# Expert retrieval of 64 of 256 tokens moved from the dense product to indirect row fetches; the first dense table in unsplit fp32

## The chip, the cores and the metric

One NeuronCore of a Trainium2 chip runs the whole layer. The metric is the device time of one execution in microseconds; of several runs the median is taken. The engines are PE (TensorE, matrix products), DVE (VectorE), ACT (ScalarE), POOL (GpSimd) and SP (SyncE, which here only issues DMAs). They run side by side and meet in semaphores.

## What is computed

The reference is one transformer layer over 256 latent tokens of width 1024 with 256 context tokens beside them. After the mixers and the output projection comes the part that the change is about, an expert layer (PEER): each token picks, for each of 8 heads, 16 of 16384 experts, each of which is one row of a table `peer_u` and one row of a table `peer_v`.

```
s = einsum('thpd,hpkd->thpk', h2 @ w_q, sub_keys)      # 2 lists of 128 scores for each head
top 16 of each list, their 256 sums, top 16 of these   -> expert (t, 8, 16), best_s
g   = softmax(best_s)
act = gelu(einsum('thkd,td->thk', u_tab[expert], h2))
out = einsum('thk,thkd->td', g * act, v_tab[expert])
x   = rmsnorm(x + g2 * out)
```

All of it is in fp32, and both tables are 16384 x 1024, 64 MB each.

## The kernel before, in words

The kernel doesn't fetch rows. It streams both tables whole and multiplies them by all 256 tokens, and a matrix of gates, zero nearly everywhere, picks out the experts that a token chose. A table is cut into 128 chunks of 128 rows (512 KB each), and SP brings each chunk into one of the four slots of `stage`.

The order of the work on each engine is written out by hand, in the order of the program text, and every engine runs its list strictly in that order:

- **Prologue** (to about 319 us). Modulation, input projection, attention, output projection, then `w_q` blocks 0 to 7, whose products become queries, and `keys(h)`, which scores the keys of head h. `schedule()` lists these steps for PE, ACT and DVE. POOL computes the low halves of the last five `w_q` blocks. DVE starts on the choice of experts while PE is still at the later `w_q` blocks: `choose(h, ...)` finds the best 16 of two lists of 128 and then the best 16 of 256 sums, for head h and both halves (128 tokens each) of the tokens.
- **u stage** (chunks 0 to 63 of `peer_u`). A product in full fp32 takes two passes on PE at half speed. So each operand is split in a high and a low half of type fp32r, which PE takes in one pass: ACT writes `hi` from `stage` (`round_chunk`), DVE writes `lo = stage - hi` (`rest`), and PE makes three products, hi x hi, hi x lo and lo x hi, for each of the eight blocks of 128 of the contraction (`u_chunk`: 24 matmuls with 256 columns). ACT turns the result into gelu and puts it in `A3[:, c, :]`. DVE goes on with the choice for heads 4 to 7, with one `rest` between any two of its steps, then finds the chosen indices (`BIG`, "decode"), and with ACT the softmax. At chunk `TURN_AT` (60) PE transposes the indices and gates.
- **Merge stage** (chunks 64 to 127 of `peer_u`). For each group of `GT` = 4 tokens ACT and DVE build two one-hot matrices for each token (`one1_...`, `one2`), PE multiplies them (`gates`, four fp32 products of 128x128x128), and DVE multiplies the 4x128 gates into `A3` (`gate`). There are 64 groups for the 64 chunks left, one beside each chunk. DVE also multiplies each late chunk into its place (`multiply`).
- **v stage** (128 chunks of `peer_v`). Again in split form: ACT writes `w_hi` from `A3` (`w_round`), DVE `w_lo` (`w_rest`), and for each half of the tokens and each half of the 1024 columns PE makes three products of 512 columns (`v_chunk`: 12 matmuls), summed over all chunks in banks 4 to 7.
- **Tail.** DVE adds `g2` times the sum to x (`residual`), ACT and DVE make the last norm, and SP stores.

The lines that the text below speaks of: `u_chunk` matmuls are L788 to L790, `gates` L798, `v_chunk` L851 to L853; ACT's rounding of stage L939 and of A3 L1117; DVE's `rest` L1306, `one2` L1495, `gate` L1503, `w_rest` L1535, `residual` L1561; the first step of `choose` L1261, its sums L1277; the decode L1454 to L1463; POOL's subtraction L1594 and its memsets L1598 and L1600.

Of the kernel before, what the change touches and what calls it, by code (L numbers as in the profile page):

```python
# [12 lines left out]
P = 128  # L33
D = 1024
# [19 lines left out]
PIECE = D // 2  # L54
PIECES = 4
GT = 4
GROUPS = T // GT


EARLY = 4  # L60
BESIDE = 8
TOPK_UNTIL = BESIDE * (PH - EARLY)
DECODE_UNTIL = TOPK_UNTIL + 24
SOFTMAX_UNTIL = DECODE_UNTIL + 4
TURN_AT = SOFTMAX_UNTIL
# [17 lines left out]
def schedule():  # L83
# [81 lines left out]
    for b in range(PH):  # L165
        steps.append(("w_q", b))
        turn()
        if b == 6:
            steps.append(("first_chunks", 0))
# [34 lines left out]
def bank_uses(steps):  # L204
# [12 lines left out]
    for kind, n in steps:  # L217
# [27 lines left out]
        elif kind in ("squares", "split", "context", "ctx_squares", "yn", "quarter", "first_chunks"):  # L245
# [10 lines left out]
def build(nc, x_t, ctx_t, cols, rows, sgu_gain, final_gain, constants, sgu_wt, bias_mask, ada_w, w_in,  # L256
          w_out, w_q, subkeys_t, peer_u_t, peer_v, out):
# [20 lines left out]
    with ExitStack() as stack:  # L278
# [10 lines left out]
        with ExitStack() as views:  # L289
            def view(name, size):  # L290
                return views.enter_context(nc.sbuf_tensor(name, [P, size], F32R))
# [12 lines left out]
        A = sbuf("A", [P, CHUNKS * T])  # L304
        A3 = A[:, :].rearrange("p (c t) -> p c t", t=T)

# [49 lines left out]
        assert 24576 == SCRATCH * T  # L356
# [7 lines left out]
        hi = sbuf("hi", [P, PIECES, PIECE], F32R)  # L364
        lo = sbuf("lo", [P, PIECES, PIECE], F32R)
# [4 lines left out]
        x1n = sbuf("x1n", [P, TB, D])  # L370
        YN_lo = yn_low[:, :].rearrange("p (k t) -> p k t", k=KD)
# [13 lines left out]
        w_hi = h2_hi[:, 0:2, :]  # L385
        w_lo = h2_lo[:, 0:2, :]
# [10 lines left out]
        choice_t = sbuf("choice_t", [P, 3, T])  # L397
        gelu_buf = choice[:, 0:2, :, :].rearrange("p n b t -> p n (b t)")
        con = sbuf("con", [P, 5 * P + 2])
        ident, ones, group_ones, iota, row_ones = (con[:, n * P:(n + 1) * P] for n in range(5))  # L400
        row_pick = con[:, 5 * P:5 * P + 2]
        colv = sbuf("colv", [P, COLS])
# [37 lines left out]
        hi_made, lo_made, piece_done, a_made = map(sem, ("hi_made", "lo_made", "piece_done", "a_made"))  # L440
# [32 lines left out]
        def _(sp):  # L473
# [33 lines left out]
            with sp.Fori(1, CHUNKS // SLOTS) as i:  # L507
                for j in range(SLOTS):
                    sp.wait_ge(lo_made, i * (2 * SLOTS) + (2 * (j + 1 - SLOTS)))
                    sp.dma_start(stage[:, j, :], peer_u_t[i * SLOTS + j]).then_inc(stage_full[j], 16)  # L510
            with sp.Fori(0, CHUNKS // SLOTS) as i:
                for j in range(SLOTS):
                    sp.wait_ge(lo_made, i * (2 * SLOTS) + (2 * (CHUNKS + j + 1 - SLOTS)))
# [11 lines left out]
        def _(pe):  # L525
# [192 lines left out]

            def queries(b):
# [21 lines left out]
            for kind, n in steps:  # L741
# [24 lines left out]
                elif kind in ("squares", "split", "context", "ctx_squares", "yn", "quarter", "first_chunks"):  # L766
# [907 lines left out]
```

## Time and profile before

| | |
|---|---|
| three runs | 1107.93 us median (1102.68 to 1108.59) |
| profiled execution, first to last instruction | 1106.2 us |
| PE busy | 1072.4 us, 97% |
| DVE, ACT, POOL busy | 760.1, 628.5 and 37.1 us |
| HBM read | 190 MB, 173 GB/s over the span |
| chunks 0 to 63 of peer_u | 319.4 to 505.7 us |
| chunks 64 to 127 with the gates | 505.7 to 746.9 us |
| peer_v | 748.0 to 1096.5 us |

The profile was taken of an execution of its own, and what is known of its time is its span; it lies within the three runs, 1.7 us under their median. Matmuls are pipelined: a matmul's own duration in the profile (283 ns for one of 256 columns) is longer than the distance from its start to the start of the next one, and it is the distance that adds up.

### The profile page before, as it was taken

The page shows a single profiled execution, that of the slowest core. Times are in us where ns is not written, and L with a number is a line of the kernel's source. Part 1 is how long each engine was busy: PE and PEld are TensorE (multiplying, and loading weights), DVE is VectorE, ACT ScalarE, POOL GpSimd, SP SyncE. Part 2 cuts the span into 40 slices and gives each one's busy share as a digit, 9 for nine tenths or more (in the row PEclk, how much of TensorE's full clock was granted, in tenths as well). Part 3 has the DMA queues.
Part 4 walks back from the last instruction along what each step waited for, and adds up shares of the span by engine and source line. Part 5 has one row for each costly group of instructions (what it writes and reads, how often), then busy time and mean ns, then how long its engine had stood idle before and what let it go on. Part 6 is the DMA issues. An engine that isn't in the chain of part 4 may idle for free.

```text
span 1106.2 us, 22735 instructions
## 1 busy us (share of the span) xinstructions
PE 1072.4 (97%) x7358; PEld 962.5 (87%) x7358; DVE 760.1 (69%) x1660; ACT 628.5 (57%) x1319; POOL 37.1 (3%) x11
## 2 busy tenths in 40 slices
PE   5899999999999999999999999999999999999996
PEld 3687986797999999999999999997888888888885
DVE  1373145576988878868888888886666666666666
ACT  2452235545345555578888888875555555555554
POOL 0000000003340000020000000000000000000000
PEclk9698998999999999999999999999999999999998
DMA  9665741044525555555344344445555666666653
GB/s 362 274 234 197 268 159 57 1 154 152 228 78 190 175 188 173 187 183 161 133 140 144 133 140 144 133 133 174 196 197 192 190 191 192 194 197 192 190 191 113
DMA packets 45547, 191.65 MB, mean 173 GB/s; under 512 B 5186, under 2 KB 5314, under 8 KB 38980
## 3 DMA queue, kind: packets, MB, share of 16 engines
q1 hardware_dynamic: 45508, 191.11, 50.9%
q8 instruction: 26, 0.43, 0.2%
q14 instruction: 13, 0.11, 0.0%
HBM read 190.04 MB, written 1.05 MB: 173 GB/s over the span
## 4 chain that ended last, share of the span: by engine, by line
PE 92%; ACT 3%; DMA 2%; DVE 2%; POOL 0%; issue 0%; DVEq 0%; SPq 0%; ACTq 0%
PE bank L788 11%; PE bank L789 11%; PE bank L790 11%; PE bank L851 10%; PE bank L853 10%; PE bank L852 10%; PE bank L798 5%; PE bank L546 3%; PE bank L547 3%; PE bank L548 3%; PE bank L669 2%; PE bank L566 1%; PE bank L652 1%; PE bank L651 1%; PE bank L660 1%; PE bank L556 1%
## 5 line engine op out<-in xcount | busy, mean ns | idle before, releaser
L939 ACT ACTIVATE hi<-stage 128x512 fp32r<-128x512 f32 x512 | 305.7, 622 | 119.6 <-PE bank L790 119.5
L1306 DVE TENSOR_TENSOR lo<-stage,hi 128x512 fp32r<-128x512 f32 x512 | 336.2, 695 | 33.9 <-ACT hi L939 31.4
L788 PE MATMUL bank<-h_hi,hi 128*128 128x256 f32 x1024 | 295.1, 288 | 1.0 <-ACT A L1062 1.0
L790 PE MATMUL bank<-h_hi,lo 128*128 128x256 f32 x1024 | 289.6, 283 | 0.0
L789 PE MATMUL bank<-h_lo,hi 128*128 128x256 f32 x1024 | 289.5, 283 | 0.0
L851 PE MATMUL bank<-hi,h_hi 128*128 128x512 f32 x512 | 199.3, 389 | 1.2 <-DVE h_lo L1535 1.2
L853 PE MATMUL bank<-hi,h_lo 128*128 128x512 f32 x512 | 199.2, 389 | 0.0
L852 PE MATMUL bank<-lo,h_hi 128*128 128x512 f32 x512 | 199.2, 389 | 0.0
L788 PEld LDWEIGHTS bank<-h_hi,hi 128*128 128x128 f32 x1024 | 196.1, 192 | 1.1 <-ACT A L1062 1.1
L789 PEld LDWEIGHTS bank<-h_lo,hi 128*128 128x128 f32 x1024 | 196.3, 192 | 0.0
L790 PEld LDWEIGHTS bank<-h_hi,lo 128*128 128x128 f32 x1024 | 196.0, 191 | 0.0
L1117 ACT ACTIVATE h_hi<-A 128x256 fp32r (+1 forms) x128 | 53.5, 418 | 162.4 <-PE bank L853 159.5
L1535 DVE TENSOR_TENSOR h_lo<-A,h_hi 128x256 fp32r<-128x256 f32 x128 | 54.5, 426 | 129.4 <-ACT h_hi L1117 129.4
L851 PEld LDWEIGHTS bank<-hi,h_hi 128*128 128x128 f32 x512 | 96.1, 188 | 21.2 <-issue 1.4
L852 PEld LDWEIGHTS bank<-lo,h_hi 128*128 128x128 f32 x512 | 96.1, 188 | 20.1
L853 PEld LDWEIGHTS bank<-hi,h_lo 128*128 128x128 f32 x512 | 96.1, 188 | 19.9
L1081 ACT ACTIVATE gate_buf<-con,choice_t 128x128 f32<-128x128 f32 x256 | 81.2, 390 | 0.0
L548 PE MATMUL bank<-h_hi,ring_low 128*128 128x256 f32 x256 | 72.6, 284 | 0.0
L1495 DVE TENSOR_SCALAR gate_buf<-con,choice_t 128x128 f32<-128x128 f32 x256 | 71.0, 340 | 0.0
L798 PE MATMUL bank<-gate_buf 128*128 128x128 f32 x512 | 67.6, 275 | 0.0
L798 PEld LDWEIGHTS bank<-gate_buf 128*128 128x128 f32 x512 | 62.8, 192 | 0.0
L1503 DVE TENSOR_TENSOR A<-A,bank 128x512 f32 (+1 forms) x64 | 43.9, 687 | 10.4 <-PE bank L798 1.8
(222 smaller groups left out, 1365.8 us busy)
## 6 DMA issues: line engine op xcount, KB each, us to landing
stage<-in_peer_u_t SPq DMA_DIRECT2D x128, 512.0 KB, 3.3
stage<-in_peer_v SPq DMA_DIRECT2D x128, 512.0 KB, 3.6
A<-in_ada_w SPq DMA_DIRECT2D x24, 1024.0 KB, 7.5
A<-in_w_in SPq DMA_DIRECT2D x11, 1024.0 KB, 4.8
A<-in_w_q SPq DMA_DIRECT2D x8, 1024.0 KB, 5.2
A<-in_w_out SPq DMA_DIRECT2D x4, 1024.0 KB, 7.3
stage<-in_bias_mask SPq DMA_DIRECT2D x1, 2048.0 KB, 12.9
A<-in_x_t SPq DMA_DIRECT2D x1, 1024.0 KB, 5.3
```

What stands on the lines that cost most here:

```text
L548: mm = pe.matmul(o, a_lo, b_hi, start=False, stop=(k == KD - 1))
L788: pe.matmul(o, hi[:, p, kk], h2_hi[:, k, :], start=(k == 0), stop=False)
L789: pe.matmul(o, hi[:, p, kk], h2_lo[:, k, :], start=False, stop=False)
L790: mm = pe.matmul(o, lo[:, p, kk], h2_hi[:, k, :], start=False, stop=(k == KD - 1))
L798: mm = pe.matmul(bank[4 + j][:, t * NK:(t + 1) * NK], ONE1[:, j, t, :], ONE2[:, j, t, :], start=True, stop=True)
L851: pe.matmul(o, w_hi[:, j % 2, tt], hi[:, p, :], start=first, stop=False)
L852: pe.matmul(o, w_hi[:, j % 2, tt], lo[:, p, :], start=False, stop=False)
L853: mm = pe.matmul(o, w_lo[:, j % 2, tt], hi[:, p, :], start=False, stop=last)
L939: act.activation(hi[:, (2 * j + h) % PIECES, :], stage[:, j, h * PIECE:(h + 1) * PIECE], ACT.Copy)\
L1081: last = act.activation(ONE1[:, j % 2, t, :], iota, ACT.Square, bias=choice_t[:, 0, bass.ds(g * GT + t, 1)])
L1306: dve.tensor_tensor(lo[:, p, :], stage[:, j, h * PIECE:(h + 1) * PIECE], hi[:, p, :].bitcast(F32), ALU.subtract).then_inc(lo_made, 1)
L1495: last = dve.tensor_scalar(ONE2[:, j % 2, t, :], iota, choice_t[:, 1, bass.ds(tt, 1)], choice_t[:, 2, bass.ds(tt, 1)], ALU.is_equal, ALU.mult)
```

## The change

192 tokens (`ND`) stay in the dense product, and the last 64 take another way. These 64 are two sets (`SUBS`) of 32 (`SUB`).

- **Rows.** 32 tokens with 128 experts each are laid out as 128 partitions with 32 columns: partition q*32+t holds experts of token t. Once the second half of the tokens has its experts (`expert`), POOL copies the indices into that layout (eight small DMAs) and issues an indirect DMA for each column: 128 rows of 4 KB, one for each partition, 512 KB in all. There are 64 such gathers of `peer_u` and 64 of `peer_v`, in a ring of four buffers. DVE multiplies and sums a gathered row of `peer_u` with the token's row of h2 (`row_dots`, one instruction with 1024 elements), and adds a weighted row of `peer_v` to a running sum (`row_sums`, one instruction too). h2 in row form comes from PE (`rows_turned`, four steps between `w_q` 3 and 4).
- **Order on DVE.** `choose` now takes two heads of one half of the tokens, so that the second half can be finished first. 64 `row_dots` stand between the steps of the choice for the first half, and all of them ahead of the first `one2`. The 64 `row_sums` stand in the merge stage (three of four groups, from group 14) and in the v stage (every third chunk).
- **u.** PE multiplies `stage` itself by `H2` in unsplit fp32, 192 columns. `round_chunk` and `rest` of `peer_u` fall away, and with them `first_chunks`; SP's slot comes free when PE has read it.
- **Gates.** 48 groups; merging starts at chunk 80 (`MERGE` = 128 - 48).
- **v.** The first 128 tokens as before with three products. The other 64 share a matmul: the high and the low half of their weights stand side by side as 128 stationary columns, so two products do. That makes 10 matmuls in place of 12. In the end the two halves and the row sums are folded by fp32 products.
- **Memory.** A moves by 8192 elements. `v_hi` and `v_lo` have four buffers of a whole row.

```diff
-EARLY = 4
-BESIDE = 8
-MERGE = 64
-SCRATCH = 96
+SUB = 32
+SUBS = 2
+ND = T - SUB * SUBS
+ND1 = ND - P
+ROWS = PH // 4 * TOPK
+DOTS = SUBS * ROWS
+GROUPS = ND // GT
+MERGE = CHUNKS - GROUPS
+SCRATCH = (24576 - A_AT) // ND
+EXP_AT = 44
+TURN_AT = 60
+GELU_AT = 12
+WEIGH_AT = 14
...
+        if b == 3:
+            steps += [("rows_turned", n) for n in range(2 * SUBS)]
...
+        gathered = [A[:, a:a + D] for a in (2048, 3072, 6144, 7168)]
...
+            def turned_rows(n):
+                o = opened(pe, ("rows_turned", n))
...
+                    for q in range(4):
+                        mm = pe.matmul(o[q * SUB:(q + 1) * SUB, m * P:(m + 1) * P], H2[:, k, tokens], ident,
+                                       start=True, stop=True, tile_position=(0, q * SUB))
...
-            def u_chunk(j, c):
-                o = bank[j % SLOTS][:, 0:T]
-                for h in range(2):
-                    pe.wait_ge(lo_made, c * 2 + (h + 1))
-                    for n in range(KD // 2):
-                        k, p, kk = KD // 2 * h + n, (2 * j + h) % PIECES, slice(n * P, (n + 1) * P)
-                        pe.matmul(o, hi[:, p, kk], h2_hi[:, k, :], start=(k == 0), stop=False)
-                        pe.matmul(o, hi[:, p, kk], h2_lo[:, k, :], start=False, stop=False)
-                        mm = pe.matmul(o, lo[:, p, kk], h2_hi[:, k, :], start=False, stop=(k == KD - 1))
-                    mm.then_inc(piece_done, 1)
+            def u_chunk(j, fill):
+                o = bank[j % SLOTS][:, 0:ND]
+                pe.wait_ge(stage_full[j % SLOTS], fill)
+                for k in range(KD):
+                    mm = pe.matmul(o, stage[:, j % SLOTS, k * P:(k + 1) * P], H2[:, k, 0:ND],
+                                   start=(k == 0), stop=(k == KD - 1))
+                mm.then_inc(u_read, 1)
...
+                        if tb == 0:
+                            pe.matmul(o, w1[:, 0:P], v_hi[j][:, hh], start=first, stop=False)
+                            pe.matmul(o, w1[:, 0:P], v_lo[j][:, hh], start=False, stop=False)
+                            mm = pe.matmul(o, w2[:, 0:P], v_hi[j][:, hh], start=False, stop=last)
+                        else:
+                            pe.matmul(o, w12, v_hi[j][:, hh], start=first, stop=False)
+                            mm = pe.matmul(o, w12, v_lo[j][:, hh], start=False, stop=last)
...
+            for half in range(2):
+                hh = slice(half * 512, half * 512 + 512)
+                for s in range(SUBS):
+                    rows = slice(ND1 + s * SUB, ND1 + (s + 1) * SUB)
+                    pe.matmul(bank[half][rows, :], fold4, sums[s][:, hh], start=True, stop=True,
+                              tile_position=(0, ND1 + s * SUB))
+            for half in range(2):
+                hh = slice(half * 512, half * 512 + 512)
+                pe.wait_ge(rest_out, half + 1)
+                pe.matmul(bank[half][0:ND1, :], fold2, rest[:, hh], start=True, stop=True,
+                          tile_position=(0, 0)).then_inc(folded, 1)
...
+            def row_dots(n):
+                s, c = n // ROWS, n % ROWS
+                g = gathered[n % GATHER]
+                dve.wait_ge(row_full[n % GATHER], 16 * (n // GATHER + 1))
+                dve.tensor_tensor_reduce(g, g, h2_rows[:, s, :], 1.0, 0.0, ALU.mult, ALU.add, row_dot[:, s, c:c + 1])\
+                   .then_inc(row_used, 1)
...
+                    dve.scalar_tensor_tensor(sums[s][:, :], g, w, sums[s][:, :], ALU.mult, ALU.add)\
+                       .then_inc(row_used, 1)
...
+            choose(TB - 1, PH - 2, lambda at: None)
+            decode(TB - 1, lambda: None)
+            dve.scalar_tensor_tensor(expert, choice[:, 0, TB - 1, :], float(NK), choice[:, 1, TB - 1, :],
+                                     ALU.mult, ALU.add).then_inc(expert_ready, 1)
+            for h in range(2, PH, 2):
+                choose(0, h, lambda at: row() if h > 2 or at > 3 else None)
+            decode(0, row)
             dve.sem_inc(scratch_free, 1)
+            row()
             dve.wait_ge(exped, 1)
...
+            row(12)
...
+            row(DOTS - rows_done[0])
...
+                if g == WEIGH_AT:
+                    weigh_rows()
+                if g >= WEIGH_AT and g % 4 < 3:
+                    row()
...
+            for v in range(2, CHUNKS):
+                w_rest(v)
+                if v + 2 < CHUNKS:
+                    rest_of_v(v + 2)
+                if v % 3 == 2:
+                    row()
...
+            def gather(n):
+                s, c, slot = n % DOTS // ROWS, n % ROWS, n % GATHER
+                if n >= GATHER:
+                    pool.wait_ge(row_used, n + 1 - GATHER)
+                pool.indirect_dma_start(gathered[slot], None, peer_u if n < DOTS else peer_v,
+                                        bass.IndirectOffsetOnAxis(ap=row_expert[:, s, c:c + 1], axis=0))\
+                    .then_inc(row_full[slot], 16)
...
+            pool.wait_ge(expert_in, 16 * 4 * SUBS)
+            for n in range(32):
+                gather(n)
             pool.wait_ge(scratch_free, 1)
             pool.memset(A3[:, SCRATCH:CHUNKS, :], 1.0).then_inc(ones_made, 1)
+            for n in range(32, DOTS):
+                gather(n)
```

## Rows read from the trace of the kernel before

**Rows 1.** Page, part 1: busy time, share of the span, instructions.

```profile
PE 1072.4 (97%) x7358; PEld 962.5 (87%) x7358; DVE 760.1 (69%) x1660; ACT 628.5 (57%) x1319; POOL 37.1 (3%) x11
```

**Rows 2.** Busy time by stretch; behind POOL: granted clock, DMA share, GB/s.

```profile
300.00:304.00 4.00, 3.77 (x31) 2.19 (x31) 3.90 (x25) 3.17 (x5) 3.97 (x2) 1.00 1.03 421
319.40:505.70 186.30, 185.33 (x1546) 185.16 (x1545) 152.75 (x363) 107.86 (x207) 13.90 (x2) 1.00 0.54 176
505.70:746.90 241.20, 241.14 (x2049) 240.94 (x2047) 212.48 (x503) 196.18 (x503) 0.00 (x0) 1.00 0.43 139
748.00:1096.50 348.50, 348.43 (x1536) 288.31 (x1536) 218.98 (x385) 187.20 (x385) 0.00 (x0) 1.00 0.58 188
```

**Rows 3.** Waits of PE from 319 to 1097 us: total, times, longest.

```profile
PE bank L851 <- DVE h_lo L1535: 1.2, 1, 1.2
PE bank L788 <- ACT A L1062: 1.0, 1, 1.0
```

**Rows 4.** Timeline of PE: start, duration, line, count.

```profile
247.24 3.85 PE L708 MATMUL bank<-A,con 128*128 128x256 f32 x16
252.76 1.07 PE L566 MATMUL bank<-A,csil 128*32 128x256 f32 x16
...
641.22 1.05 PE L798 MATMUL bank<-gate_buf 128*128 128x128 f32 x8
...
644.98 1.06 PE L798 MATMUL bank<-gate_buf 128*128 128x128 f32 x8
```

**Rows 5.** Timeline of PE's weight loads for unsplit fp32 products.

```profile
247.12 1.61 PEld L708 LDWEIGHTS bank<-A,con 128*128 128x128 f32 x8
...
701.36 0.98 PEld L798 LDWEIGHTS bank<-gate_buf 128*128 128x128 f32 x8
```

**Rows 6.** DVE by line and shape: busy us, mean ns, idle before.

```profile
L1306 DVE TENSOR_TENSOR lo<-stage,hi 128x512 fp32r<-128x512 f32 x512 | 336.2, 695 | 33.9 <-ACT hi L939 31.4
L1495 DVE TENSOR_SCALAR gate_buf<-con,choice_t 128x128 f32<-128x128 f32 x256 | 71.0, 340 | 0.0
L1535 DVE TENSOR_TENSOR h_lo<-A,h_hi 128x256 fp32r<-128x256 f32 x128 | 54.5, 426 | 129.4 <-ACT h_hi L1117 129.4
L1503 DVE TENSOR_TENSOR A<-A,bank 128x512 f32 x60 | 41.2, 687 | 8.5
...
L1454 DVE TENSOR_TENSOR A<-A,con 128x2048 f32<-128x2048 uint32 x4 | 9.1, 2285 | 0.0
...
L1573 DVE SCALAR_TENSOR_TENSOR x1n<-x1n,fsum,gate_buf 128x512 f32<-128x512 f32 x4 | 2.8, 746 | 0.1
```

**Rows 7.** ACT by line and shape, same columns.

```profile
L939 ACT ACTIVATE hi<-stage 128x512 fp32r<-128x512 f32 x512 | 305.7, 622 | 119.6 <-PE bank L790 119.5
...
L1117 ACT ACTIVATE h_hi<-A 128x256 fp32r x124 | 51.8, 418 | 156.1 <-PE bank L853 156.1
```

**Rows 8.** Timeline of DVE: two first steps of `choose`, its sums once, `residual`.

```profile
272.11 3.90 DVE L1277 TENSOR_TENSOR A<-top_v 128x256 f32<-128x256 f32 x2
...
290.90 0.87 DVE L1261 MAX8 top_v<-A 128x8 f32<-128x128 f32 x4
...
301.08 0.87 DVE L1261 MAX8 top_v<-A 128x8 f32<-128x128 f32 x4
...
1097.15 0.68 DVE L1561 TENSOR_TENSOR A<-bank,g2b 128x512 f32<-128x512 f32 x1
```

**Rows 9.** Timeline of POOL; its second subtraction.

```profile
270.79 4.59 POOL L1594 TENSOR_TENSOR ring_low<-A,query_hi 128x2048 fp32r<-128x2048 f32 x1 [1.54 <-ACT query_hi L956]
```

**Rows 10.** POOL by line and shape: the second memset.

```profile
L1600 POOL MEMSET A<- 128x8192 f32 x1 | 7.0, 6954 | 148.2 <-DVEq L1465 148.2
```

**Rows 11.** Page, part 6: DMA issues, count, KB each, us to landing.

```profile
stage<-in_peer_u_t SPq DMA_DIRECT2D x128, 512.0 KB, 3.3
stage<-in_peer_v SPq DMA_DIRECT2D x128, 512.0 KB, 3.6
```

More of the change, by code:

```diff
@@ L256, in build @@
 def build(nc, x_t, ctx_t, cols, rows, sgu_gain, final_gain, constants, sgu_wt, bias_mask, ada_w, w_in,
-          w_out, w_q, subkeys_t, peer_u_t, peer_v, out):
+          w_out, w_q, subkeys_t, peer_u_t, peer_u, peer_v, out):
     steps, splits = schedule()
@@ L363, in build @@
         BM = bias[:, :, :].rearrange("p s d -> p (s d)").rearrange("p (h b n) -> p h b n", h=HEADS, b=TB)
-        hi = sbuf("hi", [P, PIECES, PIECE], F32R)
-        lo = sbuf("lo", [P, PIECES, PIECE], F32R)
+        hi = sbuf("hi", [P, 2, D], F32R)
+        lo = sbuf("lo", [P, 2, D], F32R)
+        with ExitStack() as views:
+            sums = []
+            for n in range(SUBS):
+                view(f"below_sum{n}", D)
+                sums.append(view(f"sum{n}", D, F32))
         h2_hi = sbuf("h2_hi", [P, KD, T], F32R)
@@ L859, in _ @@
+                if not last:
+                    mm.then_inc(v_read, 1)
             pe.wait_ge(gated, GROUPS)
             pe.wait_ge(choice_t_ready, 2 * TB)
-            for j in range(4):
+            for j in range(SLOTS):
                 v_chunk(j, j, first=(j == 0))
-            with pe.Fori(1, CHUNKS // 4 - 1) as i:
-                for j in range(4):
-                    v_chunk(j, i * 4 + j)
+            with pe.Fori(1, CHUNKS // SLOTS - 1) as i:
+                for j in range(SLOTS):
+                    v_chunk(j, i * SLOTS + j)
@@ L1043, in _ @@
                            .then_inc(free_sem(name), 1)
-                elif kind == "first_chunks":
-                    for c in range(2):
-                        round_chunk(c, 16)
+                elif kind == "rows_turned":
+                    o = full(act, (kind, n))
+                    act.activation(h2_rows[:, n // 2, n % 2 * 512:n % 2 * 512 + 512], o[:, :], ACT.Copy)\
+                       .then_inc(free_sem((kind, n)), 1)
                 elif kind == "w_q":
@@ new lines, in gate_steps @@
+            def gate_steps(i, j):
+                one1_squares(j, i * SLOTS + j)
+                one1_rest(j, i * SLOTS + j)
+                gelu_beside(j, i * SLOTS + j)
+            with act.Fori(1, GELU_AT // SLOTS) as i:
+                for j in range(SLOTS):
+                    gate_steps(i, j)
+            act.wait_ge(row_used, DOTS)
+            act.activation(row_dot[:, :, :], row_dot[:, :, :], ACT.Gelu_apprx_tanh).then_inc(row_gelu, 1)
+            with act.Fori(GELU_AT // SLOTS, GROUPS // SLOTS - 1) as i:
+                for j in range(SLOTS):
+                    gate_steps(i, j)
@@ new lines, in _, with row, weigh_rows @@
+            rows_done = [0]
+            def row(count=1):
+                for _ in range(count):
+                    n = rows_done[0]
+                    if n < DOTS:
+                        row_dots(n)
+                    elif n < 2 * DOTS:
+                        row_sums(n)
+                    rows_done[0] += 1
+            def weigh_rows():
+                dve.wait_ge(row_gelu, 1)
+                dve.wait_ge(gate_in, 16 * 4 * SUBS)
+                link(dve.tensor_tensor(row_gate[:, :, :], row_gate[:, :, :], row_dot[:, :, :], ALU.mult))
@@ new lines, in _ @@
+            dve.wait_ge(a_made, MERGE)
+            for g in range(GROUPS):
+                if g >= 2:
+                    dve.wait_ge(gates_done, g - 1)
+                one2(g, g)
+                if g:
+                    dve.wait_ge(multiplied, g - 1)
+                    gate(g - 1, g - 1)
+                    dve.wait_ge(gated, g)
+                    multiply(g - 1, g - 1)
+                if g == WEIGH_AT:
+                    weigh_rows()
+                if g >= WEIGH_AT and g % 4 < 3:
+                    row()
@@ new lines, in _ @@
+            dve.wait_ge(multiplied, GROUPS - 1)
+            gate(GROUPS - 1, GROUPS - 1)
+            rest_of_v(0)
+            dve.wait_ge(gated, GROUPS)
+            multiply(GROUPS - 1, GROUPS - 1)
+            w_rest(0)
+            rest_of_v(1)
+            w_rest(1)
+            rest_of_v(2)
+            rest_of_v(3)
+            for v in range(2, CHUNKS):
[4 more added lines that the diff above has]
+                    row()
```

424 lines of the change are left out of this document (202 added, 222 removed).

## The prediction

> **What bounds the kernel now.** I read the busy shares first: PE 97% of the span, DVE 69%, ACT 57%, POOL 3% [rows 1]. A share is an average over stages, so next come the stretches. In all three table stages PE is busy throughout at the full clock (1.00, 2.4 GHz), while DVE is busy for 82%, 88% and 63% and the DMA engines for 43 to 58% [rows 2]. The waits of PE confirm it: two, of 1.2 and 1.0 us, in 780 us [rows 3]. So any time taken off PE here is time off the kernel, until the next thing is late. That will be DVE, or the transfers.
>
> What a PE product costs follows from the stretches. Chunks 0 to 63: 186.3 us less 0.7 for the transposes and 1.0 of waiting, over 64 x 24 matmuls, is 0.120 us each, 2.88 us for a chunk. The v stage: 348.5 / (128 x 12) = 0.227 us. Merge stage: groups start 3.76 us apart (644.98 - 641.22) [rows 4], the same as 241.2 / 64 = 3.77 [rows 2]; less 2.88 this leaves 0.89 us for the gates.
>
> **What falls away on PE.**
>
> u chunk. The new one has 8 fp32 products of 192 columns, two passes each: 16 passes. No row has 192 columns, but both neighbours are there. 128 columns: eight weight loads in 0.98 us; without the last one's own 0.19, seven steps, 0.113 us each [rows 5], and 0.89 / 8 = 0.111 from the gates. 256 columns: matmuls from 247.24, eight loads from 247.12 to 248.73, the eighth starting at 248.54 with the seventh matmul, so six steps in 1.30 us, 0.217 each [rows 4, 5]. The middle is 0.164 us, 16 x 0.164 = 2.63 us. If each pass had the 13 ns over its columns that an fp32r product has (0.120 against 256 / 2.4 GHz = 0.107), it would be 0.173 and the chunk 2.77. I take 2.63, since both fp32 rows show 4 to 5 ns. 128 x (2.88 - 2.63) = 32 us (14 by the other bound).
>
> Gates. 16 groups fewer: 16 x 0.89 = 14 us.
>
> v chunk. Two matmuls fewer: 128 x 2 x 0.227 = 58 us.
>
> Together 104 us, if PE stays the bound.
>
> **What is added on PE.** `rows_turned` has 64 fp32 products into 32-column strips, 128 passes of 128 columns. The nearest is L566, also into 32-column strips but 256 columns: 16 in 1.07 us, without the last one's own 0.38 0.046 each [rows 4]. With half the columns between 0.023 and 0.046: 3 to 6 us. The weights of the following `w_q` blocks are requested when PE is through with older ones, so the delay moves that chain as well and isn't absorbed: 5 us. The tail: `residual` for the last 128 tokens started 0.7 us after PE's end (1097.15) [rows 8]; now it waits for four fold products of 512 columns (two passes of 0.43 us each; half of that if the two strips run side by side) and one of the other fold's. That is 1.7 to 3.4 plus 0.9, less the 0.7: 2 to 4 us, I take 3.
>
> **Does the choice of experts finish in time?** This is the step with most in it, because all 64 `row_dots` stand ahead of the first `one2`, and PE can't merge before. One `choose` takes 10.2 us (290.90 to 301.08) [rows 8]. DVE has the first two when the keys of head 1 are there (about 281) and ends them at 301; the third ends at 311; the fourth waits for head 5 and ends about 327, the fifth 337; the decode is six instructions of 2.3 us and small ones, 14.4 [rows 6]: indices at about 352. Eight small DMAs and their landing cost POOL some 10 us; no row shows an issue from POOL, and the sum bears 5 to 15. The first gather is out at 362 and landed 3.3 us later, if it moves like a chunk of the same 512 KB [rows 11]: 366.
>
> From there DVE has 72 us of choice, decode and waits to do with 27 dots between. A dot of 1024 elements: the nearest are 0.695 us for 512 and 2.29 for 2048 [rows 6], so 1.2 to 1.3 us. So 27 dots take at least 72 / 27 = 2.7 us each: about 440. In the middle of the gathers POOL has a memset of 7.0 us (8192 elements before [rows 10], 8256 now) once the decode ends, which costs the stream some 7 us, since only four buffers are in flight.
>
> Pace of the other dots: the transfers. Chunks ask for 524 KB in 2.63 us, 199 GB/s. From 300 to 304 us, where the first u chunks (rows of 4 KB for each partition, as a gather has) arrive back to back, the core took in 421 GB/s [rows 2]. That leaves 222 GB/s, one gather in 2.4 us. From 452 (the first gather after the memset), 31 more: 526, with the pause at the transposes 530. PE gets to chunk 80 at 319.4 + 5 + 80 x 2.63 + 0.7 = 536. So it just fits. I book 5 us for shared transfers and slips.
>
> The Trainium skill (page "DMA: Bandwidth & Descriptors", section "Where 436 GB/s comes from") puts HBM at about 358 GB/s for a core and says that it binds for reads. By it 159 GB/s would be left, 3.3 us for a gather, and the dots would end at 366 + 63 x 3.3 + 7 = 581, 45 us late. The row of 421 GB/s speaks against it, if not for long stretches; its case is rival B.
>
> **DVE and ACT afterwards.** Merge: a group is 0.89 + 2.63 = 3.52 us on PE. DVE: `one2` 4 x 0.28, gate 0.69, multiply about 0.38, a row of 0.48 + 0.54 per 512 more, 1.28 [rows 6]: 3.5 us, in three groups of four, 2.2 in the fourth. It fits with nearly nothing to spare: 2 us booked. v: a chunk is 10 x 0.227 = 2.27 us on PE. DVE: `w_rest` of 192 columns 0.36, `rest_of_v` of 1024 elements 1.2, a third of 1.28: 2.0 us, 88%. ACT (0.42 us for 256 elements, 0.62 for 512, so 0.8 ns for each more): 0.37 + 0.26 + 1.03 = 1.66 us [rows 7]. `w_rest(v)` can start 0.5 us after PE ended chunk v-2, but in every third chunk a row stands just ahead of it and ends about 1.9 us after; then 0.36 more: 2.3 against 2.27. So 0.0 to 0.1 us per chunk, up to 13 us, I take 5. The slots of `stage` leave a v chunk three periods, 6.8 us, to land, where 3.6 sufficed [rows 11]; 231 GB/s and a gather in every third chunk (76) stay under 421.
>
> What costs nothing: the ACT and DVE work of `peer_u` that falls away was hidden under PE.
>
> **Sum.** 1106.2 - 32 - 14 - 58 + 5 + 3 + 5 + 2 + 5 = 1022. The median lies 1.7 us above this execution: **1024 us**.
>
> **Rivals.**
>
> *A. As summed*, 1024 (1008 to 1044 with the bounds of the terms): chance 0.60.
>
> *B. Gathers of 3 to 3.8 us.* For it: two queues share 16 engines, and a gather also needs POOL to write out 128 row addresses while DVE runs instructions with two SBUF inputs. That the two engines get in each other's way there is visible once: two sums of 0.74 us each took 3.90 us beside a subtraction on POOL (270.79 to 275.38) [rows 8, 9]. The dots end at 373 + 63 x 3.4 = 587, 51 us late; with the 5 already booked 1070. Against: 421 GB/s. 0.20. DVE setting the pace of the v stage by 0.2 us more per chunk gives 1045 and lies between A and B: 0.06, counted with B.
>
> *C. POOL can't issue fast enough: slower than before.* If a gather costs POOL as much as its own 4.59 us instruction [rows 9], the dots end at 373 + 63 x 4.6 = 663, 127 us late, and the time is 1024 - 5 + 127 = 1146. The `row_sums` would follow in the merge stage, one in 4.7 us, just so. It decides from 373 + 63 x Q = 536 + 88, at Q = 4.0 us for a gather. For it: nothing in the trace bounds the issue of an indirect DMA but POOL's slow elementwise work. Against: only addresses are computed, 128 for a gather, not 2048 elements in each partition. 0.11.
>
> The Trainium skill (page "SBUF — State Buffer", section "SBUF: two separate sides") warns of this: while DVE runs in a two-port mode, POOL is locked out and can't write the descriptors of its DMAs, and one that takes about 0.6 us alone took about 3.1 us. By that figure the case would be B's. No row here shows a DMA issued by POOL; the dots are not copies, and DVE idles when a gather is late, which gives the port back.
>
> *D. No change within 0.5%*: only where B and C meet, 0.03.
>
> **How the numbers follow.** 0.5% is 5.5 us, about what three runs within 6 us of each other can tell from no change. Faster by more: A and B, 0.86. Same: 0.03. Slower: C, 0.11. The range takes in A's own bounds and most of B: 1008 to 1080. C stays out of it.
>
> **What would show it right or wrong.** Starts of the u matmuls 0.164 us apart (0.173: the other bound); v chunks of 2.27 to 2.37 us; the first gather landing near 366; the last `row_dots` before 540 and no idle PE ahead of the first gates. Wrong if PE idles at chunk 80 by tens of us (then look at whether the gathers are spaced by POOL or by their landing, 2.4 us or more), if DVE's wait for gathers reaches into the v stage, or if the last u chunks are late because their loads land later than 8 us after their issue.

## The result, and the profile after

The changed kernel takes **1182.41 us** (median of 4 runs, 1178.81 to 1185.28), the kernel before beside it 1107.12: ratio **1.0685**, 95% interval 1.0647 to 1.0723. It is 75 us slower; the prediction said 83 us faster. The profiled execution has a span of 1178.7 us, against 1106.2.

The page of the changed kernel, parts 1, 2 and 6: busy shares, the PE and clock rows of the 40 slices, and the time from issue to landing of the table transfers.

```profile
PE 1028.5 (87%) x6090; PEld 900.9 (76%) x6090; DVE 687.9 (58%) x1374; ACT 485.8 (41%) x1005; POOL 204.2 (17%) x155
...
PE   6799999999999999995666666666689999999997
...
PEclk9798999999999999997889888888899999999999
...
A<-in_peer_u,row_expert POOLq DMA_INDIRECT x64, 8.6
A<-in_peer_v,row_expert POOLq DMA_INDIRECT x64, 7.2
stage<-in_peer_u_t SPq DMA_DIRECT2D x128, 512.0 KB, 5.3
stage<-in_peer_v SPq DMA_DIRECT2D x128, 512.0 KB, 5.4
```

PE was busy for 97% [rows 1] and is now for 87%. A slice is 29.5 us. From the third slice to 530 us PE is at 9, then at 5 or 6 for eleven slices, and then at 8 and 9 again: one stretch, to about 866 us, and the clock sags in nearly all of these slices. That is the merge stage. No other engine is near full there, so the next view is what PE waits for.

The waits of PE over the whole span: what it waited for, us in total, times, the longest.

```profile
PE bank L824 <- ACT gate_buf L1120: 104.7, 45, 3.2
PE bank L571 <- ACT A L1017: 8.3, 1, 8.3
PE bank L824 <- DVE gate_buf L1557: 6.9, 1, 6.9
```

In [rows 3] PE waited 2.2 us in all three table stages together. Now 45 of the 48 groups have a wait of 2.3 us ahead of their gates (L824), and what ends it is ACT's relu (L1120), the last step of the first one-hot matrices. The stretches confirm the place (behind POOL: granted clock, DMA share, GB/s):

```profile
325.00:539.00 214.00, 206.93 (x1268) 205.72 (x1268) 147.16 (x365) 54.08 (x106) 89.78 (x86) 0.99 0.94 360
539.00:880.00 341.00, 229.40 (x1197) 213.11 (x1197) 144.48 (x321) 111.77 (x304) 25.39 (x26) 0.88 0.38 124
1000.00:1100.00 100.00, 99.86 (x429) 78.94 (x428) 79.88 (x101) 63.32 (x130) 28.47 (x15) 1.00 0.89 301
```

The u and the v stage look as predicted. In the merge stage, where PE was busy throughout [rows 2], it works for 229 of 341 us at a mean clock of 0.88; DVE is at 42%, ACT at 33%, the DMA engines at 38%. No engine and no queue is full, which points to an order, not to a bound. The timeline of two groups (PE, ACT and DVE; in brackets the idle time before, and who ended it):

```profile
639.90 0.33 ACT L1106 ACTIVATE choice<-bank 128x192 f32<-128x192 f32 x1 [5.52 <-PE bank L815]
...
640.12 1.26 ACT L1114 ACTIVATE gate_buf<-con,choice_t 128x128 f32<-128x128 f32 x4
...
641.42 0.63 ACT L1120 ACTIVATE gate_buf<-gate_buf 128x512 f32<-128x512 f32 x1
642.10 1.16 PE L824 MATMUL bank<-gate_buf 128*128 128x128 f32 x8 [2.24 <-ACT gate_buf L1120]
643.10 2.77 PE L815 MATMUL bank<-A,stage 128*128 128x192 f32 x16
...
645.90 0.33 ACT L1106 ACTIVATE choice<-bank 128x192 f32<-128x192 f32 x1 [3.85 <-PE bank L815]
...
646.42 1.28 ACT L1114 ACTIVATE gate_buf<-con,choice_t 128x128 f32<-128x128 f32 x4 [0.20 <-issue]
...
647.73 0.63 ACT L1120 ACTIVATE gate_buf<-gate_buf 128x512 f32<-128x512 f32 x1
...
648.42 1.87 PE L824 MATMUL bank<-gate_buf 128*128 128x128 f32 x8 [2.55 <-ACT gate_buf L1120]
650.08 3.75 PE L815 MATMUL bank<-A,stage 128*128 128x192 f32 x16
```

Read it as a circle. ACT idles for 3.85 us until PE has finished the chunk (its gelu, L1106). Only then does it build the one-hot matrices of the next group (L1114, L1120), which were needed as soon as the chunk was done; PE idles for those 2.2 to 2.6 us. The first group shown takes 6.3 us. In the next the same 8 passes of the gates take 1.87 us in place of 1.16 and the chunk 3.75 in place of 2.77. The granted clock says why: 1.00 in the first group, and 0.54 in the first 3.1 us of the second, so for most of them PE was at the lower of its two levels (1.2 GHz):

```profile
642.10:648.40 6.30, 3.76 (x24) 3.47 (x24) 2.76 (x6) 2.24 (x6) 0.24 (x1) 1.00 0.27 92
648.40:651.50 3.10, 3.08 (x13) 3.08 (x14) 1.43 (x4) 0.00 (x0) 0.69 (x1) 0.54 0.62 205
```

Most groups alternate between 6.0 to 6.3 and 7.5 to 7.8 us; the mean of all is 6.91.

In the kernel before, ACT's gelu stood at the same place in its list, but for the chunk two back, which PE had long finished. In the changed one it is for the group's own chunk, with a wait for it. The description of the change ahead of the prediction doesn't mention this edit. Its main lines:

```diff
             def gelu_beside(j, n, reused=True):
...
+                act.wait_ge(u_read, n + (MERGE + 1))
...
-                    gelu_beside(j + 2, i * SLOTS + (j - 2))
...
+            def gate_steps(i, j):
+                one1_squares(j, i * SLOTS + j)
+                one1_rest(j, i * SLOTS + j)
+                gelu_beside(j, i * SLOTS + j)
```

### The profile page after: what moved, and what is told of

It reads as the page before. It is cut to its first block, busy times and chain, and to the rows that moved or that the text cites. A ratio compares the mean times of both kernels' runs of the same rounds, so it can differ in the third digit from the quotient of the medians.

```text
span 1178.7 us, 17862 instructions
## 1 busy us (share of the span) xinstructions
PE 1028.5 (87%) x6090; PEld 900.9 (76%) x6090; DVE 687.9 (58%) x1374; ACT 485.8 (41%) x1005; POOL 204.2 (17%) x155
## 4 chain that ended last, share of the span: by engine, by line
PE 77%; ACT 9%; DMA 7%; issue 3%; DVE 2%; POOL 1%; ACTq 1%; DVEq 0%; SPq 0%
PE bank L815 25%; PE bank L824 6%; PE bank L874 6%; PE bank L876 5%; PE bank L875 5%; PE bank L879 5%; PE bank L880 5%; ACT gate_buf L1114 4%; DMA A<-in_peer_u,row_expert 4%; PE bank L561 3%; PE bank L562 3%; PE bank L563 3%; ACT gate_buf L1120 2%; PE bank L684 1%; DMA A<-in_w_in 1%
## 5 line engine op out<-in xcount | busy, mean ns | idle before, releaser
L815 PE MATMUL bank<-A,stage 128*128 128x192 f32 x2048 | 361.1, 338 | 0.2 <-DMA stage<-in_peer_u_t 0.2
L815 PEld LDWEIGHTS bank<-A,stage 128*128 128x128 f32 x2048 | 353.2, 201 | 1.1 <-DMA stage<-in_peer_u_t 0.6
L1660 POOL DMA_INDIRECT A<-in_peer_v,row_expert x64 | 95.8, 1497 | 489.2 <-DVE sum L1361 379.7
L824 PE MATMUL bank<-gate_buf 128*128 128x128 f32 x384 | 76.2, 360 | 116.2 <-ACT gate_buf L1120 104.7
L824 PEld LDWEIGHTS bank<-gate_buf 128*128 128x128 f32 x384 | 64.7, 255 | 130.3 <-ACT gate_buf L1120 118.0
L1349 DVE CUSTOM_DVE_ANT_0 A<-A 128x1024 f32<-128x1024 f32 x64 | 77.9, 1222 | 59.4 <-DMA A<-in_peer_u,row_expert 59.1
L1106 ACT ACTIVATE choice<-bank 128x192 f32<-128x192 f32 x48 | 15.8, 330 | 228.7 <-PE bank L815 228.7
L1384 DVE TENSOR_TENSOR v_lo<-stage,v_hi 128x1024 fp32r<-128x1024 f32 x64 | 78.3, 1223 | 31.0 <-ACT v_hi L975 30.7
L1384 DVE TENSOR_TENSOR lo<-stage,hi 128x1024 fp32r<-128x1024 f32 x64 | 78.2, 1222 | 27.2 <-ACT hi L975 26.8
L1660 POOL DMA_INDIRECT A<-in_peer_u,row_expert x64 | 69.2, 1081 | 96.5 <-DVE row_dot L1349 91.2
L1361 DVE SCALAR_TENSOR_TENSOR sum<-A,row_gate,sum 128x1024 f32<-128x1024 f32 x62 | 79.3, 1278 | 0.0
L975 ACT ACTIVATE hi<-stage 128x1024 fp32r<-128x1024 f32 x64 | 67.1, 1048 | 10.2 <-DMA stage<-in_peer_v 10.2
L975 ACT ACTIVATE v_hi<-stage 128x1024 fp32r<-128x1024 f32 x64 | 67.1, 1049 | 9.9 <-DMA stage<-in_peer_v 9.7
L1114 ACT ACTIVATE gate_buf<-con,choice_t 128x128 f32<-128x128 f32 x192 | 60.8, 390 | 1.3 <-issue 1.3
```

Of the source, the lines that this page charges most:

```text
L815: mm = pe.matmul(o, stage[:, j % SLOTS, k * P:(k + 1) * P], H2[:, k, 0:ND], start=(k == 0), stop=(k == KD - 1))
L824: mm = pe.matmul(bank[4 + j][:, t * NK:(t + 1) * NK], ONE1[:, j, t, :], ONE2[:, j, t, :], start=True, stop=True)
L975: act.activation(v_hi[j], stage[:, j, :], ACT.Copy).then_inc(hi_made, 1)
L1114: last = act.activation(ONE1[:, j % 2, t, :], iota, ACT.Square, bias=choice_t[:, 0, bass.ds(g * GT + t, 1)])
L1349: dve.tensor_tensor_reduce(g, g, h2_rows[:, s, :], 1.0, 0.0, ALU.mult, ALU.add, row_dot[:, s, c:c + 1])\
L1361: dve.scalar_tensor_tensor(sums[s][:, :], g, w, sums[s][:, :], ALU.mult, ALU.add)\
```

## Experiments

The theory (T): this order on ACT is the whole loss. Rivals: DVE (R1), the transfers (R2), ACT short of time whatever its order (R3). What each expects of a run stands ahead of what was measured.

**e1_act_order.** ACT builds the matrices of group g+1 ahead of the gelu of group g. Nothing else moves.

```diff
+            one1_squares(0, 0, reused=False)
+            one1_rest(0, 0)
             for j in range(SLOTS):
-                one1_squares(j, j, reused=j >= 2)
-                one1_rest(j, j)
+                one1_squares(j + 1, j + 1, reused=j >= 1)
+                one1_rest(j + 1, j + 1)
                 gelu_beside(j, j, reused=j >= 2)
...
```

> The changed kernel with one edit on ACT: in the merge stage the one-hot matrices of group g+1 are built ahead of the gelu of chunk 80+g, not behind it. Theory T (ACT's order is the loss: the gelu waits for the end of the u chunk, and the matrices that the next gates need stand behind it): groups start 3.5 to 3.7 us apart in place of 6.0 to 7.7, PE's clock stays at its full level, the merge stage takes 170 to 180 us in place of 343, and the time is 1010 to 1022 us. Rival R1 (DVE sets the merge stage: multiply, a row sum and one2 follow each other behind the gelu): groups 4.5 us apart or more, 1060 us or more. Rival R2 (transfers or gathers set it): no change, 1182 us.

Measured: 1027.98 us (1021.74 to 1031.5), ratio to before 0.9272 (0.922 to 0.9324). Groups are 3.49 us apart, and mostly 3.57 to 3.59 once the row sums stand among them. The median is 6 us above what T allowed. In the profiled execution the first u chunk starts 3.3 us later than in the changed kernel (323.9 against 320.6), and the row sums cost the merge stage some 3 us (e4). ACT's wait is gone from PE's list, and what is left is one wait for DVE ahead of the first gates:

```profile
PE bank L824 <- DVE gate_buf L1560: 6.0, 1, 6.0
```

**e2_pe_order.** The other side of the circle: ACT's and DVE's lists stay, PE takes the chunk first and the gates of the group behind it, so that ACT has the gates' time and a chunk's for its two steps.

```diff
-                    gates(j % 2, i * SLOTS + j)
                     pe.wait_ge(a_made, i * SLOTS + (MERGE + j + 1 - SLOTS))
                     u_chunk(j, i * 16 + (MERGE // SLOTS * 16 + 16))
+                    gates(j % 2, i * SLOTS + j)
```

> The changed kernel with one edit on PE instead: in the merge stage u chunk 80+g goes ahead of the gates of group g, so that a whole u chunk lies between the gelu and the next gates. ACT's and DVE's orders stay. Theory T: the matrices of group g+1 are ready 2.3 us after a u chunk's end, PE asks for them 0.9 + 2.6 = 3.5 us after it; groups 3.5 to 3.7 us apart, 1010 to 1025 us, the same as with ACT's order mended. If ACT were short of time rather than badly ordered (rival R3), this would not help: over 1100 us.

Measured: 1021.73 us (1017.49 to 1027.21), ratio 0.9231 (0.918 to 0.9283); beside e7 again 1022.26. The timeline of two groups in e2:

```profile
640.12 1.26 ACT L1114 ACTIVATE gate_buf<-con,choice_t 128x128 f32<-128x128 f32 x4
640.58 2.77 PE L815 MATMUL bank<-A,stage 128*128 128x192 f32 x16
...
641.41 0.63 ACT L1120 ACTIVATE gate_buf<-gate_buf 128x512 f32<-128x512 f32 x1
...
643.19 1.05 PE L824 MATMUL bank<-gate_buf 128*128 128x128 f32 x8
643.39 0.33 ACT L1106 ACTIVATE choice<-bank 128x192 f32<-128x192 f32 x1 [1.34 <-PE bank L815]
...
644.08 2.77 PE L815 MATMUL bank<-A,stage 128*128 128x192 f32 x16
```

ACT still waits for PE (1.34 us), PE for nobody: 644.08 - 640.58 = 3.50 us for a group. Work, engines and transfers are those of the changed kernel, and 161 us are gone. That leaves no room for R1, R2 and R3 beyond a few us.

**e3_act_more.** The opposite: a second relu on ACT (a no-op in value, 0.65 us) behind the first in each group of the changed kernel.

```diff
...
-                act.activation(ONE1[:, j % 2], ONE1[:, j % 2], ACT.Relu, bias=1.0, scale=-1.0).then_inc(one1_made, 1)
+                act.activation(ONE1[:, j % 2], ONE1[:, j % 2], ACT.Relu, bias=1.0, scale=-1.0).then_inc(one1_once, 1)
+                act.wait_ge(one1_once, g + 1)
+                act.activation(ONE1[:, j % 2], ONE1[:, j % 2], ACT.Relu).then_inc(one1_made, 1)
```

> The changed kernel with a second Relu over the finished one-hot matrices of a group, 128x512, about 0.65 us more on ACT for each of 48 groups; the values stay as they are. Theory T (ACT's matrices are the last thing that the gates wait for): each group starts 0.65 us later at the full clock, 31 us in all, and more where PE falls to the lower clock: 1210 to 1235 us. Rivals R1 and R2 (DVE or transfers): no change within 0.5%.

Measured: 1213.26 us (one run), 31 us more. The quick groups, those at the full clock, come 6.66 us apart where they came 6.01, so the 0.65 us arrives whole in each, although ACT is idle for 62% of this stage even here. That 48 x 0.65 also makes 31 is in part luck: the first u chunk starts 5.5 us later here (326.1 against 320.6), and the mean distance of the groups grew by 0.5 us (6.91 to 7.41), because fewer of them fell to the lower clock. The wait of PE grew from 2.3 to 3.0 us each:

```profile
PE bank L825 <- ACT gate_buf L1123: 134.0, 45, 3.9
```

**e4_rows_late.** e1 with all 64 row sums in the v stage, one in every second chunk.

```diff
-                if g >= WEIGH_AT and g % 4 < 3:
-                    row()
...
-                if v % 3 == 2:
+                if v % 2 == 0 or v == CHUNKS - 1:
                     row()
```

> As the kernel with ACT's order mended, but no row_sums in the merge stage: all 64 stand in the v stage, one in every second chunk. Prices DVE's share in both stages. If DVE's work sets the merge stage with its rows (3.5 us of work for a group of 3.5), groups come closer together here by 0.1 to 0.3 us (5 to 14 us in all); if PE sets it, they stay as they are, 3.5. In the v stage DVE has 0.36 + 1.22 + 0.64 = 2.2 us for a chunk of 2.27: if the order of the row ahead of w_rest costs time there, chunks take 2.3 to 2.4 us, 5 to 15 us in all.

Measured: 1024.18 us (one run, within e1's spread). Behind the first, groups are 3.49 us apart throughout, so in e1 the sums cost the merge stage 0.08 us for each group that has them beside it, 3 us in all; the v stage takes some 3 us more (302.4 against 299.1). Both are less than the 5 us that was the least expected if DVE's sums cost time there, and they cancel. R1's whole size is thus some 3 us.

**e5_before_lag0.** Is the order enough by itself? The kernel before, with the gelu of the merge stage waiting for its own chunk.

```diff
...
-                    gelu_beside(j + 2, i * SLOTS + (j - 2))
+                    act.wait_ge(piece_done, i * (2 * SLOTS) + (2 * (MERGE + j + 1)))
+                    gelu_beside(j, i * SLOTS + j)
```

> The kernel before, with ACT's order changed alone: the gelu of a chunk in the merge stage stands at the end of its own group and waits for that chunk, where it stood two chunks later. Theory (ACT waiting for PE's chunk with the next group's matrices and roundings behind it is enough by itself, without any indirect DMA or a smaller dense part): after each chunk PE waits for gelu 0.42, four squares 1.3, two roundings 1.2 (part of them behind the gates) and relu 0.64, at least 2.4 and at most 3.6 us, on 3.77 for a group: 6.2 to 7.4 at the full clock, and more with stretches of half clock. 64 groups: 1108 + 155 to 1108 + 330, so 1260 to 1440. Rival (the order only matters together with the new transfers and dots): 1105 to 1130.

Measured: 1461.4 us (one run; before 1106.59), 21 us beyond what T allowed. The wait was in its bounds, the clock wasn't. The wait of PE that is longest in sum, and then the window of its merge stage:

```profile
PE bank L798 <- ACT gate_buf L1087: 198.1, 61, 3.5
```

```profile
506.00:1100.00 594.00, 386.25 (x2044) 373.19 (x2042) 212.12 (x505) 200.10 (x511) 0.00 (x0) 0.74 0.17 56
```

The 355 us are 64 groups of 5.5 us more each. Of these 3.2 are the wait; the other 2.3 are PE's own work, 386 / 64 = 6.0 us for a group in place of 3.77, at a granted clock of 0.74. No gather, no dot, no smaller dense part is needed for the loss. Here ACT's roundings of the next chunk stand behind the wait as well, so the circle is a longer one than in the changed kernel: the run shows that the order is enough by itself, not how long the changed kernel's circle is.

**e6_after_fill.** How much of the loss is clock? The changed kernel, with six products of 192 columns in PE's idle time, into a bank that nobody reads.

```diff
+            def fill_wait():
+                for _ in range(6):
+                    pe.matmul(bank[6][:, 0:ND], ident, H2[:, 0, 0:ND], start=True, stop=True)
...
                     pe.wait_ge(gated, i * SLOTS + (j - 1))
+                    fill_wait()
                     gates(j % 2, i * SLOTS + j)
```

> The changed kernel with six more products of 192 columns on PE (2.0 us at the full clock, into a bank that nobody reads) between the end of a u chunk and the next gates, where PE waits 2.3 us for ACT. This leaves ACT's chain as it is and takes away only the idle stretch. If all of the loss is the wait of 6.0 us per group, the clock costs nothing and the time stays at 1178 to 1190. If the slow clock after the idle stretches costs what the alternation of 6.0 and 7.6 us shows, all groups come at 6.0 to 6.2 us, 48 of them in 292 us in place of 329, and the time is 1140 to 1155 although PE has 96 us more of work.

Measured: 1149.03 us (two runs, 1148.83 to 1149.24), **33 us faster with 92 us more of work** (47 x 1.96). A row of its waits, and four of its timeline:

```profile
PE bank L828 <- ACT gate_buf L1127: 17.6, 47, 1.3
```

```profile
639.72 1.16 PE L828 MATMUL bank<-gate_buf 128*128 128x128 f32 x8 [0.60 <-ACT gate_buf L1127]
...
643.32 2.11 PE L822 MATMUL bank<-A,con 128*128 128x192 f32 x12
...
645.73 1.16 PE L828 MATMUL bank<-gate_buf 128*128 128x128 f32 x8 [0.29 <-ACT gate_buf L1127]
...
651.73 1.16 PE L828 MATMUL bank<-gate_buf 128*128 128x128 f32 x8 [0.29 <-ACT gate_buf L1127]
```

Behind the first and up to the last, groups now start 6.00 to 6.31 us apart (6.13 in the mean of all), at a granted clock of 0.99. The 6.00 is also what the quick groups of the changed kernel take, so ACT's chain is as it was, and 6.00 is the pure length of the circle. From the first gates to the last the changed kernel takes 324.9 us, e6 288.1 and e2 165.6. That splits the loss in this stage, 159 us: 37 go with the lower clock (the medians differ by 33, but e6's first u chunk also starts 4.6 us later), and 122 are the wait, 47 x (6.00 - 3.49) = 118 and 4 of scatter.

**e7_one2_early.** What is left in e2 is a wait of 3 to 4 us ahead of the first gates: the last dots end on DVE at about 535, and `one2` stands behind them. Here `one2` of groups 0 and 1 stands ahead of the last dots.

```diff
...
+            dve.wait_ge(choice_t_ready, 2 * TB)
+            one2(0, 0)
+            one2(1, 1)
             row(DOTS - rows_done[0])
...
```

> PE's order as in e2, and DVE builds the second one-hot matrices of groups 0 and 1 before its last dots. In e2 PE waited 3.2 us there and ran about one group at half clock behind it (2.05 us for the gates, 1.2 more than usual, and about 0.6 more in the chunk). Theory (the last piece of time that the dots cost is that they stand ahead of one2): the wait is gone and the clock stays up, 4 to 6 us less than e2, so 1015 to 1019. Rival: the dots end at 535.5 and the gate of group 0 on DVE then comes later than PE needs it for gates(2), so the wait moves there and nothing is gained: 1021 to 1023.

> The kernel of e2 once more, beside e7 on the same chip, so that a difference of some us can be told: 1018 to 1025.

Measured: **1018.25 us** (1015.95 to 1020.26, 5 runs), ratio 0.9194 (0.9176 to 0.9212); e2 on the same chip 1022.26, ratio 0.924 (0.9223 to 0.9258). The intervals don't touch, and 4.0 us is what the theory allowed. No wait ahead of the first gates is left among PE's waits. Of the versions that compute the whole layer it is the fastest here, 8.1% under before.

**e8_quarter_rows.** e2 with 1 KB in place of 4 KB for each row fetched (another row's address; the 64 tokens come out other than the reference's). As many gathers, dots and sums; the dots write their products into `sums` (an edit not shown here), and the first four gathers fetch whole rows.

```diff
-                pool.indirect_dma_start(gathered[slot], None, peer_u if n < DOTS else peer_v,
+                w, table = D if n < GATHER else D // 4, peer_u if n < DOTS else peer_v
+                if n >= GATHER:
+                    table = table.rearrange("e (a b) -> (e a) b", b=w)
+                pool.indirect_dma_start(gathered[slot][:, 0:w], None, table,
...
```

> e2 with a quarter of the bytes in each gather: 256 elements of a row instead of 1024 (the address names another row; the first four are whole, and the dots write their products elsewhere). As many gathers, dots and sums as before, so the output is not the reference's for the 64 tokens. If the gathers are paced by their bytes beside the u chunks (the prediction's pace of 2.4 us each), the dots of the second half follow DVE's or POOL's pace of 1.1 to 1.5 us, end near 490, and PE's wait ahead of the first gates (3.2 us with its slow clock, about 5 in all) is gone: 1014 to 1018, stage loads back from 5.3 towards 3.3 us. If the gathers are paced by POOL's issue or by the four buffers' round trip whatever their size, they stay at 2.5 us each and the time stays at 1020 to 1023.

Measured: 1014.53 us (1013.46 to 1016.84), 7.7 us under e2 on the same chip; no wait ahead of the first gates; `stage` loads of `peer_u` land after 4.2 us (5.6 in e2 on the same chip). The stretch from 460 to 530 us in e2 and then in e8:

```profile
460.00:530.00 70.00, 70.00 (x433) 69.84 (x434) 35.29 (x61) 17.87 (x34) 30.31 (x34) 1.00 1.01 400
```

```profile
460.00:530.00 70.00, 70.00 (x435) 69.98 (x434) 32.13 (x56) 17.89 (x34) 37.13 (x35) 1.00 0.78 252
```

In e2 the 16 DMA engines are full at 400 GB/s. With a quarter of the bytes the last dot starts at 521.4 instead of 534.3, not at 490. DVE had its twelve dots done at 462.7 and then idled for 17 us, up to PE's transposes at chunk 60, with 24 dots behind them:

```profile
479.81 0.29 DVE L1547 TENSOR_SCALAR choice_t<-bank 128x128 f32<-128x128 f32 x1 [17.09 <-PE bank L841]
```

These 24 came 1.77 us apart; the same 24 in e2 came 2.38 us apart. So the bytes set a good part of that pace and not all of it; what sets the rest is not shown. The two windows also allow an estimate of what a gather takes, with 26 and 27 of them issued: the 27 u chunks in 70 us take 0.50 of the DMA time at 400 GB/s, so a gather of long rows takes the 16 engines (1 - 0.5) x 70 / 26 = 1.3 us and one of short rows (0.78 - 0.5) x 70 / 27 = 0.7 us, more than half for a quarter of the bytes.

## Why the prediction was wrong, by its own steps

**The step that failed** is the one under "DVE and ACT afterwards. Merge: a group is 0.89 + 2.63 = 3.52 us on PE. DVE: ... It fits with nearly nothing to spare". It adds up what DVE has to do in a group, and stops. ACT's sum would have been small, 0.33 + 1.27 + 0.63 = 2.2 us, and a sum wouldn't have found the fault: the work fits well within 3.52 us and still stalls. What was missing is the order, with waits, on ACT: `gelu_beside` now waits for chunk 80 + g, and the matrices of group g + 1, which PE wants right behind that chunk, stand behind it. The change adds this wait, and for an added wait one has to name what is queued behind it on its engine. It was done for POOL and DVE, not for ACT. No rival had it: the slower one was C, an issue rate of POOL, and C did not happen. Measured, the group takes 6.91 us in place of 3.52, with 2.3 us of PE waiting for ACT in it.

The other steps can be read off e2, which differs from the changed kernel only in PE's order of chunk and gates, and so is free of the circle. Its span is 1019.2; the sum said 1022.

| term | said | measured |
|---|---|---|
| u and merge stages | -39 (-32 - 14 + 5 + 2) | 427.5 to 383.2: -44 |
| between u and v | 0 | 1.1 to 2.7: +2 |
| v stage | -53 (-58 + 5) | 348.5 to 300.9: -48 |
| `rows_turned` | +5 | first u chunk 319.4 to 320.5: +1 |
| tail | +3 | 9.7 to 11.9: +2 |
| sum | -84 | -87 |

- **u chunk** 2.63 us: right. In the changed kernel ACT's gelus at the end of the u stage start 2.60 us apart:

```profile
525.32 0.33 ACT L1099 ACTIVATE A<-bank 128x192 f32 x1 [0.99 <-PE bank L815]
527.92 0.33 ACT L1099 ACTIVATE A<-bank 128x192 f32 x1 [2.27 <-PE bank L815]
530.52 0.33 ACT L1099 ACTIVATE A<-bank 128x192 f32 x1 [2.27 <-PE bank L815]
```

  So a pass of 192 columns takes 2.60 / 16 = 0.163 us, the middle of the two neighbours in [rows 5]; the 13 ns of fp32r don't apply.
- **Gates, groups of 3.52 us**: 3.49 in e2. **v chunk**: 2.27 us was said, 300.9 / 128 = 2.35 is the mean; the 5 us for DVE's order should have been 10. e8 gives 2.5 of them back, with fewer bytes.
- **`rows_turned`**, 5 us: not settled. First chunks start between 318.2 and 326.1 us in the nine kernels here with this prologue, 322.3 in the mean, and at 319.4 and 319.0 in the two without `rows_turned`. So the 1 us of e2 is one draw of a spread of 8 us.
- **The first gather** was said to land at 366. It landed by 362.4, where the first dot starts. POOL issues it at 356.58, 5 us earlier than the 362 said, and it landed about 5.8 us later where 3.3 was said:

```profile
350.01 4.16 POOL L1669 DMA_DIRECT2D row_expert<-A  x8 [23.93 <-DVE A L1526]
356.58 1.01 POOL L1660 DMA_INDIRECT A<-in_peer_u,row_expert  x1 [2.41 <-DMA row_expert<-A]
357.90 0.96 POOL L1660 DMA_INDIRECT A<-in_peer_u,row_expert  x1 [0.30 <-issue]
```

  The eight small DMAs took 6.6 us with their landing, not 10.
- **Pace of the dots, and rivals B and C.** Said 2.4 us for a gather at 421 GB/s; the last dots of the changed kernel start 2.4 to 2.6 us apart, each after a gather's landing, at 360 GB/s over the stretch and 400 in e2's later part. The last dot ends at 535.9, 6 us later than the 530 said. PE reaches chunk 80 at 530.4 in place of 536, which turns "it just fits" into a wait of 6.9 us, and a first group at half clock behind it. B's 3 to 3.8 us for a gather did not come; the dots were late as it said, by 6 us and not by 51. C needed 4.0 us of POOL for each:

```profile
L1660 POOL DMA_INDIRECT A<-in_peer_v,row_expert x64 | 95.8, 1497 | 489.2 <-DVE sum L1361 379.7 <-DVE sum L1358 101.6 <-issue 7.0
L1361 DVE SCALAR_TENSOR_TENSOR sum<-A,row_gate,sum 128x1024 f32<-128x1024 f32 x62 | 79.3, 1278 | 0.0
L1349 DVE CUSTOM_DVE_ANT_0 A<-A 128x1024 f32<-128x1024 f32 x64 | 77.9, 1222 | 59.4 <-DMA A<-in_peer_u,row_expert 59.1 <-DVE choice L1522 0.2
...
L1660 POOL DMA_INDIRECT A<-in_peer_u,row_expert x64 | 69.2, 1081 | 96.5 <-DVE row_dot L1349 91.2 <-issue 2.9 <-DMA row_expert<-A 2.4
```

  It takes 1.1 to 1.5 us in the mean. The dot and the sum are 1.22 and 1.28 us, as said (1.2 to 1.3 and 1.28).
- **The two pages of the Trainium skill** that the prediction weighed. The page "DMA: Bandwidth & Descriptors", section "Where 436 GB/s comes from", would have put the dots' end at 581; the changed kernel's trace has 535.9, and e2's has 400 GB/s sustained over 70 us, above the 358 that the section gives for a core. The page "SBUF — State Buffer", section "SBUF: two separate sides", warned of POOL's descriptors waiting for DVE, 3.1 us in place of 0.6. The trace agrees in kind: 88 of the changed kernel's 128 issues took 0.93 to 1.14 us, and the other 40 took 1.62 to 2.75. Each of these 40 ended 0.80 to 0.85 us after the end of a DVE instruction that ran beside it and had both its inputs in SBUF. One of them (L1515 is a step of the decode):

```profile
417.51 2.29 DVE L1515 TENSOR_TENSOR A<-A,con 128x2048 f32<-128x2048 uint32 x1
417.86 2.75 POOL L1660 DMA_INDIRECT A<-in_peer_u,row_expert  x1 [1.74 <-DVE row_dot L1349]
```

  So what B feared of POOL and DVE is real. It cost little here: 34 of the 40 are gathers of `peer_v`, ahead of which POOL is idle for 5.4 us in the mean, and the last dots waited for landings.

So each row of the table held within 5 us and the sum within 3, the latter partly by luck: the v stage was 5 us dearer than said and the u and merge stages 5 us cheaper, and the start of the u stage alone scatters by 8 us. A single wait whose queue nobody had followed turned 83 us of gain into 75 of loss.

## What to carry to other kernels

On an engine that works in order, a wait's price isn't its instruction but everything that stands behind it: for each stage write one period's list for every engine, the idle ones too, and ask of each entry whether the next engine needs it before or after the event that the entry ahead of it waits for. One changed place in one list removed the circle here (e1, e2). A lag of a stage or two between a product and its consumer keeps it away in the kernel before (the gelu of chunk c-2; e5 takes the lag out and loses 355 us); in the changed kernel the lag wasn't tried. The sign of it in a profile is a stretch in which no engine and no queue is full, PE's waits all have the same length and the same releaser, and that releaser is itself waiting for PE.

## What the runs showed of the hardware

- Idle times of PE of 2.3 us once in 6 to 8 us cost clock as well: the granted clock was 0.88 in the merge stage, and the same chunk took 2.77 or 3.75 us by turns. With the idle time cut to 0.3 to 0.6 us by products that nobody needs (e6) it was 0.99, and the kernel 33 us faster. With waits of 3.2 us in groups of 9.3 (e5) it was 0.74.
- fp32 passes of 192 columns start 0.163 us apart, on the line between 0.111 for 128 and 0.217 for 256 [rows 5]; products of fp32r have 0.120 for 256 [rows 2], so with 192 columns in two passes the unsplit product costs 0.326 us against 0.36 for three fp32r products of 256.
- A gather of 128 rows of 4 KB held POOL for 0.93 to 1.14 us in 88 of 128 cases. In the other 40 it held it for 1.62 to 2.75 us, to 0.80 to 0.85 us behind the end of a DVE instruction with two inputs in SBUF. The table transfers and the gathers together drew 400 GB/s with all 16 DMA engines full. Gathers of 1 KB rows left them 78% busy at 252 GB/s: by e8's working, an estimate, 0.7 us of all 16 engines for 128 rows of 1 KB, 1.3 us for 128 of 4 KB.
